# Matrix-memory attention: squares and squared denominators summed on VectorE, one product with ones per head

## The reference

```
num = (s_qk weighted by gates) @ v                     # per token a row of 128 values
den = sum over keys of the weighted s_qk
h   = num / max(|den|, exp(-m_t))
hm  = rms_norm(h, ml_norm)                             # mean of squares over the 128 values, EPS = 1e-6
y   = sigmoid(o) * hm
```

## Time and profile before

| | |
|---|---|
| median of 3 runs | 2498.09 us (2497.86 to 2499.7) |
| profiled execution | 2499.32 us, span 2497.6 us |
| PE busy | 2473.6 us (99%), 13524 instructions |
| PEld busy | 2081.4 us (83%) |
| DVE busy | 1419.3 us (57%), 1935 instructions |
| ACT busy | 1041.0 us (42%), 1547 instructions |
| POOL busy | 985.2 us (39%), 729 instructions |

### The profile page before, as it was taken

The page is one execution under the profiler, slowest core; times in us unless marked ns, Lnnn a source line. Parts: engine busy times, 40 slices in busy tenths (PEclk is TensorE's granted clock), DMA queues, the critical chain, the costliest instruction groups (busy, mean ns, idle before and its releaser), DMA issues.

```text
span 2497.6 us, 37091 instructions
## 1 busy us (share of the span) xinstructions
PE 2473.6 (99%) x13524; PEld 2081.4 (83%) x13524; DVE 1419.3 (57%) x1935; ACT 1041.0 (42%) x1547; POOL 985.2 (39%) x729
## 2 busy tenths in 40 slices
PE   9999999999999999999999999999999999999999
PEld 8999999957777789988777788888887578888887
DVE  6988114376446678841596755653355955666213
ACT  5556324375334445542565332222244743222222
POOL 3001553403224430055353655554453045556443
PEclk9999999999999999999999999999999999999999
DMA  4333333202112233333321232323232122232322
GB/s 162 99 104 97 110 102 105 79 1 60 60 59 96 91 101 103 105 116 97 104 96 48 93 101 93 100 92 99 95 127 82 57 90 99 95 101 93 110 93 85
DMA packets 72188, 230.96 MB, mean 92 GB/s; under 512 B 9298, under 2 KB 9554, under 8 KB 72083
## 3 DMA queue, kind: packets, MB, share of 16 engines
q1 hardware_dynamic: 64128, 216.27, 26.8%
q10 hardware_dynamic: 7954, 13.26, 1.7%
HBM read 220.58 MB, written 5.24 MB: 90 GB/s over the span
## 4 chain that ended last, share of the span: by engine, by line
PE 94%; DVE 4%; ACT 1%; issue 0%; DMA 0%; POOL 0%; SPq 0%; DVEq 0%; ACTq 0%
PE PS L305 24%; PE PS L307 24%; PE PS L306 24%; PE PS L819 5%; PE PS L821 5%; PE PS L820 5%; PE PS L2221 1%; DVE ast__155 L3490 1%; DVE asx L3510 1%; PE PS L1863 0%; PE PS L2247 0%; PE PS L1844 0%; PE PS L2882 0%; PE PS L2233 0%; PE PS L2893 0%
## 5 line engine op out<-in xcount | busy, mean ns | idle before, releaser
L299 POOL TENSOR_TENSOR wlo<-wraw,whi 128x512 fp32r<-128x512 f32 (+2 forms) x354 | 466.3, 1317 | 1450.8 <-ACT whi L291 1450.8
L305 PE MATMUL PS<-xh,whi 128*128 128x512 f32 (+1 forms) x1672 | 621.1, 371 | 4.2 <-POOL wlo L300 1.9
L307 PE MATMUL PS<-xh,wlo 128*128 128x512 f32 (+1 forms) x1672 | 614.1, 367 | 0.0
L306 PE MATMUL PS<-xl,whi 128*128 128x512 f32 (+1 forms) x1672 | 613.9, 367 | 0.0
L291 ACT ACTIVATE whi<-wraw 128x1024 fp32r<-128x1024 f32 (+2 forms) x354 | 354.5, 1003 | 592.9 <-PE PS L307 578.7
L300 POOL TENSOR_TENSOR wlo<-wraw,whi 128x512 fp32r<-128x512 f32 (+2 forms) x354 | 528.7, 1494 | 0.0
L305 PEld LDWEIGHTS PS<-xh,whi 128*128 128x128 f32 x1672 | 313.4, 187 | 61.1 <-issue 3.0
L307 PEld LDWEIGHTS PS<-xh,wlo 128*128 128x128 f32 x1672 | 313.4, 187 | 52.7
L306 PEld LDWEIGHTS PS<-xl,whi 128*128 128x128 f32 x1672 | 313.4, 187 | 52.2 <-issue 1.4
L305 PE MATMUL PS<-hid2h,whi 128*128 128x512 f32 x560 | 218.4, 390 | 0.0
L306 PE MATMUL PS<-hid2l,whi 128*128 128x512 f32 x560 | 217.9, 389 | 0.0
(11 more groups left out here) (549 smaller groups left out, 5036.7 us busy)
## 6 DMA issues: line engine op xcount, KB each, us to landing
wraw<-w_up_dram SPq DMA_DIRECT2D x96, 512.0 KB, 3.3
wraw<-w_dn_dram SPq DMA_DIRECT2D x48, 512.0 KB, 3.3
wraw<-w_f1gu_dram SPq DMA_DIRECT2D x44, 512.0 KB, 3.3
wraw<-w_f2gu_dram SPq DMA_DIRECT2D x44, 512.0 KB, 3.2
wraw<-w_hyin_dram SPq DMA_DIRECT2D x24, 512.0 KB, 3.3
wraw<-w_win_dram SPq DMA_DIRECT2D x18, 512.0 KB, 3.3
wraw<-w_gate_dram SPq DMA_DIRECT2D x16, 512.0 KB, 3.3
wraw<-w_pg_dram SPq DMA_DIRECT2D x16, 512.0 KB, 3.3
```

The source lines that it names most:

```text
L299: pool.tensor_tensor(wlo[:, s, 0:half], wraw[:, s, 0:half], whi[:, s, 0:half].bitcast(F32), ALU.subtract)
L305: pe.matmul(out_, whi[:, s, a:b], xhi, start=start, stop=False, skip_group_check=True)
L306: pe.matmul(out_, whi[:, s, a:b], xlo, start=False, stop=False, skip_group_check=True)
L307: return pe.matmul(out_, wlo[:, s, a:b], xhi, start=False, stop=stop, skip_group_check=True)
```

## The change

`larger` gets a second VectorE instruction, which adds `msq` to `mden` in place. The signal `mx` counts both, so it is raised twice per head and its waits are renumbered. `squares` and `last_squares` multiply ones by `mden` alone, one product in place of two that add up in PSUM. `squares(hd-1)` moves from unit j = 1, behind the spread, to unit j = 2, behind the sums.

```diff
-                "st", s=16, m=4, w=16, st=16, cut=16, pv=16, nm=4, abs=4, mx=4, sq=4, ss=4, ln=4,
+                "st", s=16, m=4, w=16, st=16, cut=16, pv=16, nm=4, abs=4, mx=8, sq=4, ss=4, ln=4,
...
                     if hd >= 2:
-                        pe.wait_ge(*mx_done(hd - 1))
+                        pe.wait_ge(*mx_done(2 * hd - 3))
...
                 def squares(hd):
-                    pe.wait_ge(*sq_done(hd + 1))
-                    pe.wait_ge(*mx_done(hd + 1))
-                    pe.matmul(PS3[:, 6 + hd % 2, :], c_("ones"), msq[:, :], start=True, stop=False,
-                              skip_group_check=True)
-                    pe.matmul(PS3[:, 6 + hd % 2, :], c_("ones"), mden[:, :], start=False, stop=True,
+                    pe.wait_ge(*mx_done(2 * hd + 2))
+                    pe.matmul(PS3[:, 6 + hd % 2, :], c_("ones"), mden[:, :], start=True, stop=True,
                               skip_group_check=True).then_inc(ss_done.s, 1)
...
-                    if j == 1 and hd >= 1:
+                    if j == 2 and hd >= 1:
                         squares(hd - 1)
...
                     dve.tensor_tensor(mden[:, :], mden[:, :], PS3[:, 2 + hd % 2, :], ALU.max).then_inc(mx_done.s, 1)
+                    dve.wait_ge(*mx_done(2 * hd + 1))
+                    dve.wait_ge(*sq_done(hd + 1))
+                    dve.tensor_tensor(mden[:, :], mden[:, :], msq[:, :], ALU.add).then_inc(mx_done.s, 1)
...
             def last_squares(pe):
-                pe.wait_ge(*sq_done(4))
-                pe.wait_ge(*mx_done(4))
-                pe.matmul(PS3[:, 7, :], c_("ones"), msq[:, :], start=True, stop=False, skip_group_check=True)
-                pe.matmul(PS3[:, 7, :], c_("ones"), mden[:, :], start=False, stop=True,
+                pe.wait_ge(*mx_done(8))
+                pe.matmul(PS3[:, 7, :], c_("ones"), mden[:, :], start=True, stop=True,
                           skip_group_check=True).then_inc(ss_done.s, 1)
-            return st_done(16), l_done(2), l_done(4), l_done(3), last_squares, mx_done(3)
+            return st_done(16), l_done(2), l_done(4), l_done(3), last_squares, mx_done(6)
```

## The result

The changed kernel took 2501.89 us in the median of 17 runs (2499.38 to 2505.13), the kernel before 2498.1 (2496.5 to 2499.76, 17 runs): a ratio of 1.0016, 95% interval 1.0010 to 1.0022. It is 3.8 us slower where +2.4 was forecast, inside the range and inside the 0.2% that was called no change. The profiled execution took 2503.54 us for a span of 2501.4.

What follows compares the result with a forecast made beforehand. TensorE was taken to bound the kernel (94% of the chain's span), with a second loop through squares and gain equally long. +3.27 late at over keys(3) less 0.86 gave +2.4, 2500.5 us; range 2496.4 to 2503.0.

Steps and rivals of the forecast that it cites:

- The loops: Squares, ScalarE's root, VectorE's gain, next block's first `mst`: as long as TensorE's own work, so any delay of squares shows.
- Both loads: Weight loads of scores(10) and scores(14), released by `mst`; forecast to show some 1 us of idleness after the change.
- The removed work: Four `msq` products off TensorE, 0.86 us each, 3.4 us if nothing else moved; 0.86 was counted as coming back.
- The addition: Four new VectorE additions, one per head, 0.7 to 1.7 us each, starting 0.71 us after the maximum.
- The delay it gives scores(12): In block 2 scores(12) must wait for `mst` behind the addition: load at 1371.22 where squares had loaded at 1370.50.
- The port: In block 3 VectorE with two SBUF inputs and GpSimd's splits lock each other out; over keys(3) loads 3.27 us late.
- Four turns in block 3: Third addition, `yl`, `macc` 14 and `macc` 15 each alternate with a GpSimd piece, ending at 1384.99; before, only two paid.
- Rival 2: Port turns spare the new addition in block 3; over keys(3) 1.9 us late, net +1.0, 2499.1; chance 0.18.
- The clock: Rival: TensorE's clock falls on new idleness; one stretch costs 1.7 us (2502.2, chance 0.12), two make 2503.9 (0.06).
- the sum of +2.4: Whole kernel: over keys(3) 3.27 us late in block 3, less 0.86 for the product removed at the last squares.

Runs made afterwards that it cites:

- e1: The changed kernel with squares back at unit j = 1 behind the spread, one product and the addition kept; 2496.85 us, -1.3 against the kernel before.
- e2: The kernel before with only the move of squares to unit j = 2, both products kept, no added VectorE instruction; 2501.44 us.
- e9: The changed kernel with squares at unit j = 1 and the recurrence's rounding moved to the stage's start; 2496.36 us.
- e5: The changed kernel with GpSimd held before its splits of the next matrix until `yl` of head 1 is done; 2499.12 us.
- e6: The changed kernel with GpSimd's splits of the next matrix's first four chunks moved between its cuts; 2499.13 us.
- e3: The kernel before with only the addition, its result unused, both products kept and squares at unit j = 1; 2498.92 us.
- the second set: The changed kernel run again unchanged, 11 executions on another chip; 2500.85 us, +2.8 against the kernel before.
- e7: The changed kernel with squares at unit j = 1 and GpSimd's splits early; 2496.34 us, -1.6 against the kernel before.

## Why the prediction was right

**The loops.** Both loads that the prediction picked as signs of a second loop of equal length went from 0.79 and 0.50 us of idleness to 1.80 and 1.79. The reading (an engine at 99%, but with loads released by another engine, has no slack behind it) carried the whole case. e1 and e2 show it by experiment: without the move the change is 1.3 under the kernel before, with the move alone it is 3.3 above.

For scores(10) the reading named the wrong holder. The prediction took its wait in the kernel before as a sign that the loop of squares, root and gain was as long as TensorE's work. But the root of block 1 was ready there at 1365.06, and the gain started at 1365.38, behind the rounding of the recurrence in VectorE's queue:

```profile
1363.18 2.28 DVE L2844 TENSOR_TENSOR yl<-grg,yh 128x2048 fp32r<-128x2048 f32 x1
...
1364.42 0.64 ACT L2957 ACTIVATE mrb<-mrb 128x512 f32<-128x512 f32 x1
```

In the changed kernel the root ends at 1365.60, 0.54 later, and there it is the loop that decides, by 0.14 us: the prediction's 1365.52 for the gain, against the 1365.38 of the queue. So the number holds, but the sign didn't show what it was read for; e1, where squares is early, gets nothing in block 1, and e9 gets it back by moving the rounding. For scores(14) in block 2 the reading was right.

**The removed work.** 3.4 us of TensorE did go. 0.86 came back as such, at the last squares, where nothing waits.

**The addition.** 0.69 alone, 1.30 under GpSimd, inside the bounds of 0.7 to 1.7; the fourth, which nothing waits for, took 0.99. The delay it gives scores(12) is in the trace to the hundredth.

**The port.** Four turns in block 3 as worked out; e5 takes two of them away and e6 all. Rival 2 did not happen: GpSimd started 0.51 us ahead of the addition, where 0.3 had been worked out. It was a near thing: in e1 and e3, where the addition comes before GpSimd's first piece, it takes 0.69.

**The clock.** Here the size was off, in the price and in the chance. The prediction gave a clock stretch 1.7 us, with a chance of 0.12 for one and 0.06 for two; that price came from a single row with a mean of 0.66 over 5 us. The stretch of the profiled execution, seven microseconds at a mean of 0.52, cost 3.4. Half of the changed kernel's executions have less than full clock in the mean, with medians 1.6 us (at 0.999) and 3.6 us (at 0.998) above the 2500.3 of those at full clock. At full clock the sum of +2.4 is right to 0.2 us (+2.2). The other 1.6 of the 3.8 measured in the first 17 runs are not in the sum; that nine of these 17 were below full clock and so carried the median was the draw: the second set, with five of eleven, has +2.8. That the spread of the kernel before comes from window attention was argued from one row; e5's trace has such a stretch there as well, but no run tested it:

```profile
1970.00:1975.00 5.00, 3.95 (x20) 2.46 (x22) 4.86 (x17) 2.84 (x10) 0.00 (x0) 0.66 0.01 3
```

## What to carry to other kernels

Look at the loads of the busiest engine that another engine releases: each one is a second chain with no slack. Follow that chain back to what really held it: the loop itself, or another instruction in the releasing engine's queue. Work taken off the busy engine gains there only what the head of that chain gains, while issuing the head later costs the delay wherever nothing else hides it. Before work is moved to VectorE with both inputs in SBUF, look at what GpSimd runs at that time; each such instruction may wait for a whole one of GpSimd's. A change that leaves TensorE idle for some microseconds may also be paid for in its clock afterwards, in some executions only, so the median of a few can miss it.

## What the runs showed of the hardware

VectorE and GpSimd took turns in block 3, where both had instructions waiting with two SBUF inputs: 1.30, 1.75, 1.04 and 1.04 us for VectorE's 512, 512, 256 and 128 columns, where they take 0.69, 0.69, 0.42 and 0.29 alone, each followed by one piece of GpSimd. A VectorE copy from SBUF to SBUF of 128 columns, with one input, is held up as well: 0.23 us alone, 1.35 while GpSimd splits, in e7's trace:

```profile
1357.66 1.27 POOL L299 TENSOR_TENSOR wlo<-wraw,whi 128x512 fp32r<-128x512 f32 x1
1357.67 1.35 DVE L3007 COPY macc<-mst 128x128 f32<-128x128 f32 x1
```

And 2.6 us of products whose results nobody reads, placed in a wait, cost nothing that can be measured: the changed kernel's median with them is not above the one without (2500.70 for 2500.85, on two chips). The clock stood at 1.00 over the stage in the one execution that was traced.
